# Value products of the sample tokens: one wide matmul per token row in place of three 32-column tiles

## The reference, cut to what matters

```python
s = jnp.einsum('btgrd,bgtnjd->btgrnj', q, kvg[..., 0, :]) * scale
p = _masked_softmax(s.reshape(B, G, T, R, k_top * SEL_BLOCK), smask)...
o_s = jnp.einsum('bgtrnj,bgtnjd->btgrd', p.astype(q.dtype), kvg[..., 1, :])
...
o_w = jnp.einsum('btgrl,blgd->btgrd', p.astype(q.dtype), kvw[:, :, 1])
o = g[..., 0:1] * o_c + g[..., 1:2] * o_s + g[..., 2:3] * o_w
```

## Time and profile before

| | before |
|---|---|
| median of 3 runs | 933.69 us |
| the profiled execution | 941.16 us, its span 939.4 us |
| TensorE busy (matmul records) | 833.3 us, 89% |
| VectorE, ScalarE, POOL busy | 341.7, 269.6, 108.9 us |
| TensorE's share of the chain that ended last | 83% |
| mean granted TensorE clock | 0.915 |

### The profile page before, as it was taken

How to read it: one execution, slowest core, us unless ns; L and a number is a source line. 1 busy time by engine, 2 the same in 40 slices (tenths; PEclk the granted TensorE clock), 3 DMA queues, 4 the chain that set the end, 5 groups by cost and what they waited for, 6 DMA issues and landing times.

```text
span 939.4 us, 16800 instructions
## 1 busy us (share of the span) xinstructions
PE 833.3 (89%) x7021; PEld 550.3 (59%) x7021; DVE 341.7 (36%) x774; ACT 269.6 (29%) x713; POOL 108.9 (12%) x178
## 2 busy tenths in 40 slices
PE   0899999999997999989999787898968779887996
PEld 0455666666664655778784454565646667654441
DVE  0133133333333111432030364666646346433433
ACT  0135323332333000011120354565713323333211
POOL 1200600000000000000000383111131112000000
PEclk9999799999998999968999988999975876877998
DMA  9949703333000222320451016000062656520121
GB/s 229 374 195 334 287 1 135 134 134 134 0 0 1 73 71 89 93 89 2 143 220 67 7 55 284 2 2 1 1 236 76 248 192 221 208 78 31 45 79 33
DMA packets 34407, 108.09 MB, mean 115 GB/s; under 512 B 5667, under 2 KB 14930, under 8 KB 33187
## 3 DMA queue, kind: packets, MB, share of 16 engines
q1 hardware_dynamic: 28579, 56.77, 17.9%
q0 software_dynamic: 5760, 50.33, 14.2%
HBM read 101.80 MB, written 11.55 MB: 121 GB/s over the span
## 4 chain that ended last, share of the span: by engine, by line
PE 83%; DVE 6%; ACT 4%; issue 3%; SPq 2%; another core or an unknown queue 1%; DMA 0%; POOL 0%; ACTq 0%; DVEq 0%; POOLq 0%
PE ps L862 18%; PE ps L1007 13%; PE ps L1275 7%; PE ps L1005 7%; PE ps L1161 5%; PE ps L848 4%; PE ps L1061 3%; PE ps L1110 3%; PE ps L1185 3%; PE ps L1201 2%; PE ps L1085 2%; PE ps L1012 2%; PE ps L973 1%; SPq L651 1%; PE ps L808 1%
## 5 line engine op out<-in xcount | busy, mean ns | idle before, releaser
L862 PE MATMUL ps<-xt,w 128*128 128x381 f32 x512 | 175.1, 488 | 0.7 <-DVE xt L1286 0.7
L1007 PE MATMUL ps<-wcols,hT 128*128 128x384 f32 (+3 forms) x384 | 123.8, 483 | 2.1 <-DVE hT L1642 2.1
L862 PEld LDWEIGHTS ps<-xt,w 128*128 128x128 f32 x512 | 93.7, 192 | 53.6 <-issue 1.4
L1007 PEld LDWEIGHTS ps<-wcols,hT 128*128 128x128 f32 x384 | 74.0, 194 | 48.7 <-issue 30.1
L1285 DVE COPY xt<-ps 64x384 f32<-64x384 f32 x64 | 35.3, 551 | 154.9 <-PE ps L848 154.8
L1275 PE MATMUL ps<-w_o,mixT 128*128 128x512 f32 (+1 forms) x160 | 70.6, 600 | 0.0
L1161 PE MATMUL ps<-kt,qs 32*32 32x128 f32 x1920 | 51.4, 354 | 18.8 <-issue 14.2
L1285 ACT COPY xt<-ps 64x384 f32<-64x384 f32 x64 | 30.2, 472 | 124.3 <-PE ps L848 121.9
L1005 PE MATMUL ps<-hT,wcols 128*128 128x288 f32 x256 | 64.5, 413 | 0.7 <-ACT z_gate L1334 0.7
L848 PEld LDWEIGHTS ps<-ident,cache 128*128 128x128 f32 x384 | 46.2, 144 | 22.9 <-issue 13.9
L1161 PEld LDWEIGHTS ps<-kt,qs 32*32 32x32 f32 x1920 | 43.2, 129 | 27.9 <-issue 20.1
(11 more groups left out here) (290 smaller groups left out, 1004.8 us busy)
## 6 DMA issues: line engine op xcount, KB each, us to landing
wcols<-in_w_ada SPq DMA_DIRECT2D x6, 2048.0 KB, 10.7
wcols<-in_w_in SPq DMA_DIRECT2D x4, 2048.0 KB, 8.5
win_rows<-in_state_win_kv SPq DMA_DIRECT2D x8, 768.0 KB
out<-in_state_win_kv SPq DMA_DIRECT2D x1, 6048.0 KB
wcols<-in_w_in SPq DMA_DIRECT2D x2, 1536.0 KB, 12.0
w_o<-in_w_out SPq DMA_DIRECT2D x1, 3072.0 KB, 11.5
w<-in_phi_w SPq DMA_DIRECT2D x4, 512.0 KB, 9.7
x_rows<-in_x_prompt SPq DMA_DIRECT2D x1, 2048.0 KB, 8.8
```

The costliest lines, as they stand in the source:

```text
L862: last = pe.matmul(ps[:, 4 + k, 0:G * NC].rearrange("p (g n) -> p g n", g=G), w1[:, m * JP + s - 1, k, :], xt[(s - 1) % NXT][:, k * G:(k + ...
L1007: last = pe.matmul(ps[:, job_bank[j], 0:width], hT[:, c, t * P:(t + 1) * P], w[:, c, col:col + width], **flags)
```

## The change

`sample_values` makes one matmul for each token row j: all 96 columns of `pt` are the weights, and the 192 value columns of the three groups are streamed at once. The result in PSUM is 96 x 192 for each branch: the rows of group g against the values of all three groups, of which only the block of group g is wanted. The selected branch stands in columns 0:192 of bank 7, the window branch in 192:384. The new tokens take one matmul with 384 columns, and `new_v` is laid out to fit, so that each of its DMAs writes rows of 192 values in place of three pieces of 64. `finish_sample` reads the diagonal blocks, each of 32 rows by 64, with three instructions in place of L1812 and three in place of L1814.

```diff
-                    sp.dma_start(new_v[u][n * TS:(n + 1) * TS, :, n * d:(n + 1) * d], rows[b, :, 1]).then_inc(win_in[u], 16)
+                    sp.dma_start(new_v[u][n * TS:(n + 1) * TS, n, :], rows[b, :, 1].rearrange("t g d -> t (g d)")).then_inc(win_in[u], 16)
...
-                values, at0 = (win_rows[b % NBUF], d) if late else (kv_rows[(b * (NCH - 1) + c) % NROW], 0)
+                values, at0 = (win_rows[b % NBUF], G * d) if late else (kv_rows[(b * (NCH - 1) + c) % NROW], 0)
                 for j in range(4):
-                    for g in range(G):
-                        v0 = KV // 2 + g * d
-                        last = pe.matmul(ps[g * SQ:(g + 1) * SQ, 7, at0:at0 + d], pt[n % NPT][:, j, g * SQ:(g + 1) * SQ],
-                                         values[:, j, v0:v0 + d], start=(c == 0 and j == 0), stop=False, skip_group_check=True)
+                    last = pe.matmul(ps[0:GR, 7, at0:at0 + G * d], pt[n % NPT][:, j, :], values[:, j, KV // 2:],
+                                     start=(c == 0 and j == 0), stop=False, skip_group_check=True)
                 if late:
-                    for g in range(G):
-                        last = pe.matmul(ps[g * SQ:(g + 1) * SQ, 7, 0:2 * d], pt[n % NPT][0:2 * TS, 4, g * SQ:(g + 1) * SQ],
-                                         new_v[b % NBUF][:, g, :], start=False, stop=True, skip_group_check=True)
+                    last = pe.matmul(ps[0:GR, 7, 0:2 * G * d], pt[n % NPT][0:2 * TS, 4, :],
+                                     new_v[b % NBUF][:].rearrange("p n c -> p (n c)"), start=False, stop=True, skip_group_check=True)
                 last.then_inc(pt_used, 1)
...
-                own_step.done(dve.scalar_tensor_tensor(out=out_rows[u][:], in0=ps[0:GR, 7, 0:d], scalar=coef[:, 2:3],
-                                                       in1=cmp_out[:, b, :], op0=ALU.mult, op1=ALU.add))
-                dve.scalar_tensor_tensor(out=out_rows[u][:], in0=ps[0:GR, 7, d:2 * d], scalar=coef[:, 3:4],
-                                         in1=out_rows[u][:], op0=ALU.mult, op1=ALU.add).then_inc(out_made, 1)
+                for g in range(G):
+                    of = slice(g * SQ, (g + 1) * SQ)
+                    last = dve.scalar_tensor_tensor(out=out_rows[u][of], in0=ps[of, 7, g * d:(g + 1) * d], scalar=coef[of, 2:3],
+                                                    in1=cmp_out[of, b, :], op0=ALU.mult, op1=ALU.add)
+                own_step.done(last)
+                for g in range(G):
+                    of = slice(g * SQ, (g + 1) * SQ)
+                    last = dve.scalar_tensor_tensor(out=out_rows[u][of], in0=ps[of, 7, (G + g) * d:(G + g + 1) * d],
+                                                    scalar=coef[of, 3:4], in1=out_rows[u][of], op0=ALU.mult, op1=ALU.add)
+                last.then_inc(out_made, 1)
```

More of the change, by code:

```diff
@@ L321, in program @@
         win_rows = [at(f"win_rows{u}", [P, WJ, KV], win_at[u]) for u in range(NBUF)]
-        new_v = [at(f"new_v{u}", [2 * TS, G, 2 * d], win_at[u] + WJ * KV * 4) for u in range(NBUF)]
+        new_v = [at(f"new_v{u}", [2 * TS, 2, G * d], win_at[u] + WJ * KV * 4) for u in range(NBUF)]
         gate_dram = nc.dram_tensor("gate_dram", [NS, 3 * H], F32).ap()
```

## The result

The changed kernel takes 946.5 us (four runs, 945.85 to 949.22), the kernel before 932.54 us by its four runs. The ratio is 1.0155, with a 95% interval of 1.0119 to 1.019. It is slower, as forecast, by 14 us and not by 6.

What follows compares the result with a forecast made beforehand. TensorE was taken as the bound: 21 us of work added, 9.3 back from pauses and 6 from the clock, total +5.7, giving 939.4 us on the median (ratio 1.0061). Own range 933 to 946, with rivals 927 to 960.

Steps and rivals of the forecast that it cites:

- The bound: Whole stage: TensorE bounds it, so what the change does to TensorE goes to the end unless something covers it.
- Price of a value chunk: Values on TensorE: a chunk takes 1.30 us in place of 0.58 at full clock, 2.56 in place of 1.00 at half.
- Work added: Each round on TensorE: 3.9 us more per sequence, part of it filling waits, +2.8 net a round.
- The pattern round: Round from 792.01, with one clock fall: 14.21, less 0.4, plus 2.8, gives 16.6 us; six of them 99.6.
- The pauses: In the scores, TensorE out of instructions behind DMA bursts: three of four go, one of 2.5 us stays; 9.3 come back.
- The clock: Rounds of the stage: dense value streams raise the granted clock, one fall a round; 6 us come back.
- DVE and DMAs: Four more DVE instructions a sequence, 1.1 us at most, covered by waits for scores; new_v's DMAs and SP's, POOL's waits cost nothing.
- The last stretch: From 822.80 to 838.00: seventh round's 9.9 us become 10.4, the last sequence's 5.2 become 8.8; +4.1.
- Rival 3: Scores: the pauses stay, with half of the clock's return lost; +18, or 951.5 us; chance 0.11.
- Rivals 1 and 4: Stage: clock stays 1.00 and all four pauses go, 930.9 us, chance 0.22; values beside something misread, nothing moves, 934, chance 0.05.
- rival 2: Rounds: the clock falls as often as now and the values meet it; +25, or 958.5 us; chance 0.17.

Runs made afterwards that it cites:

- e3: Changed kernel with matmuls put back to three 32-column tiles, keeping the new PSUM and new_v layout and six DVE instructions: 930.78 us.
- e1: Changed kernel with a quarter of the bytes in each gather from the 15th on: 934.86 us, 1.0021 of the kernel before.
- e2: Kernel before with a quarter of the bytes in each gather from the 15th on: 918.93 us, 0.9857 of the kernel before.
- e7: Kernel before with the 4 MB of output weights issued behind sequence 6's second value chunk, not ahead of the scores of 7: 926.67 us, 0.9943.
- e9: Kernel before with the output weights issued behind sequence 6's second value chunk, measured once more with five rounds: 928.4 us, 0.9951.
- e10: Changed kernel with the output weights issued behind sequence 6's second value chunk: 944.52 us, 1.0129 of the kernel before.
- e4: Changed kernel with values 0 and 1 and turns 2 and 3 of the last sequence issued inside the scores: 942.93 us, 1.0128.
- e5: Changed kernel with values 0, 1 and turns 2, 3 inside the scores, and DVE joining a sequence straight behind the key transposes: 939.22 us, 1.0078.
- e11: Changed kernel with the wide matmul in chunks 0 and 1 alone, the rest in three narrow tiles: 945.75 us, 1.0137 of the kernel before.
- e12: Changed kernel with chunks 0 and 1 in three narrow tiles, chunks 2 to 4 and new tokens wide: 943.09 us, 1.0116 of the kernel before.
- e6: Kernel before with values 0, 1 and turns 2, 3 moved inside the scores and DVE's joining moved earlier: 949.28 us, 1.0169.
- e8: Repeat, in one look, of the changed kernel with values inside the scores and DVE joining earlier: 936.06 us.

## Why the prediction was right and wrong

**The bound, right.** The chain stayed TensorE's, and everything that the change did to it in this stage arrived at the end.

**Price of a value chunk, right.** 1.30 us at full clock, as worked out from the dense stream of rows 6. New tokens take 0.81 in place of the 0.65 expected, and the transposes behind a wide chunk 0.33 in place of 0.48, so that chunk and turn are 1.63 and not 1.78. The section is 8.65 us for the 8.8 predicted. The Trainium skill (TensorEngine Tiling (Array Packing), Key Properties) says that changing the tiling mode drains TensorE. The 0.15 us by which the pair is cheaper than the sum said is in the direction of that rule; no run here separates it from other causes.

**Work added, right.** From values 0 to the start of the next scores a round needs 10.45 us at nearly full clock (805.12 to 815.57) and 7.58 in e3 (779.30 to 786.88): +2.9 for the 2.8 predicted. What the stage grew by, with pauses and clock in it, is 19.8 us against e3 (119.1 to 138.9), for the 5.7 predicted; the span grew by 20.3 (927.2 to 947.5), the time by 15.7 (930.78 to 946.5).

**The pattern round, right in its total, by luck.** 16.6 us predicted, 16.36 measured, in the one round without a pause. The values' section was taken at 8.8 and took 10.13 (788.76 to 798.89), for its first chunk was at half clock; the rest was taken at 7.8 and took 6.23, for its scores were not. The two errors cancel. The forecast took six such rounds and got one.

**The pauses, wrong.** This is the step that failed: three of four pauses should go, because 168 instructions fewer and a later start of the scores would let the blocks in. "9.3 come back from pauses" was its term. None came back: 16.0 us in five pauses after, against 14.6 in e3 and 11.8 in the execution of rows 7. Against e3 that is 10.7 of the 14.1 us by which the stage's growth was forecast too low. The mechanism was right in part: light gathers took most of each pause away (e1, e2), the moved load of the weights took 1.6 us or more of the last (e7, e9, e10), and spreading the same instructions took most of them away (e4, e5).

Two things were wrong. The first is shown: the burst was not "nearly over by then". Over the 6 us ahead of each of the four pauses behind gathers the DMA engines of the changed kernel are 92 to 98% busy. The gathers, released later by the longer values, were still running under the scores. The second is an argument from counts: the saved instructions lie in the wrong stretch. A block is 16 KiB: 0.77 MB in 47 packets. The Trainium skill (Runtime: NRT & Kernel Launch, Instruction fetch mechanics) gives 256 instructions for it, and that agrees with the packets falling from 52 to 47 for 1,344 instructions fewer. In the changed kernel one instruction packet moves between 735.0 and 742.5 us; TensorE gets through 461 matmuls and weight loads from 735.0 on and stops at 743.01. The scores alone are 480, so that with no more than that in hand a block has to come while they run, however slowly the values in front of them use theirs. The change thinned out the stretch that had no pause and left the one that had. That section of the Trainium skill calls crossing a block mostly hidden. From 0 to 690 us TensorE's matmuls wait 2.9 us for "issue", which agrees; the 16.0 us in the scores don't.

**The clock, right in size as far as an estimate tells.** It did come back: 0.89 over the stage against 0.80 in e3 and 0.77 in the execution of rows 2. Six rounds grew by 13.0 us against e3. The added work is 6 x 2.9 = 17.4 and the pauses are 1.4 longer, so 5.8 came back by something else, and "6 from the clock" was the forecast. It came in other places than expected: the scores gained, and behind each remaining pause stands a wide chunk at half clock that takes 2.8 us, where a narrow one takes 1.00. This is an estimate from comparing rounds; no run held the clock fixed.

**DVE and DMAs, right.** Six joining instructions of 0.28 us each, as the bound from above had it:

```profile
L1811 DVE SCALAR_TENSOR_TENSOR out_rows<-ps,coef,cmp_out 32x64 f32<-32x64 f32 x24 | 6.6, 277 | 23.5 <-PE ps L1202 23.3
```

They cost nothing that can be measured (e3), and TensorE waited for them 0.3 us once. The cover was real: in e4, where the joining comes too late for values 0, TensorE waited 5.8 us for it.

**The last stretch, too small.** +4.1 predicted to the end of the values, +6.8 against e3 (14.8 to 21.5 us). The last sequence's part is 3.4 for the 3.6 worked out. The seventh round's was taken at 0.5 and is 3.4 as well (9.5 to 12.9 us): its first two chunks meet the half clock behind the pause that stays, 2.80 and 2.02 us in place of 1.30.

**The base.** The rounds were read from an execution whose part ahead of the stage was late by 6 to 12 us. That changed no term of the sum, which goes by differences, and its stage is as long as e3's.

**The rivals.** Rival 3 (the pauses stay) is the nearest to what happened, put at +18 in spans and 951.5 us with a chance of 0.11; the measured span difference is 20.3 (to e3) and the time 946.5. Its other half, pauses that have nothing to do with DMA or with instructions, doesn't fit e1, where fewer bytes, and e5, where another order took most of them away. Rivals 1 and 4 are ruled out by the time, rival 2 by the clock of 0.89.

The timed medians put the price at 14 to 16 us and the profiled spans at 20.3. Most of that gap is in the choice of executions: the changed kernel's profiled one is 2.7 us above its median, e3's 1.75 below. What stays open is why two wide chunks cost what five do. e11 and e12 bound it (9 us of added work cost 15, 12 us cost 12, with intervals that overlap) but don't say how the clock's fall is decided. How many instructions are held ahead was not tested by a run of its own.

## What to carry to other kernels

Narrow tiles side by side in the array are worth what their overlap says (here 24 ns a record against 56): a wide matmul that computes three times what is wanted saves instructions and costs the array's time, and where TensorE is the bound that is the bill. Before counting fewer instructions as a gain, look at which stretch runs out of them; taking them from another stretch returned nothing here. And look for large loads that fall on the stretch which is densest in instructions: moving one by some 9 us gave 0.5% here, at no cost.

## What the runs showed of the hardware that was not expected

- The pauses in the scores behind gathers are 2.6 to 3.4 us in the changed kernel, with DMA engines 92 to 98% busy over the 6 us ahead of each. In the scores of sequence 7 of e7, e9 and e10, with DMA engines 3% busy over the same 6 us, there is none over 0.9 us.
- TensorE, busy without a gap for 41 us with value tiles of 32 columns, was granted 0.50 throughout (e6), and 1.00 over 32 us when the value tiles were 96 columns wide in the same order (e5): being busy was not what brought the clock back.
- Two executions of one kernel had the same seven rounds to within 0.25 us, pauses and half clock included (e5, e8); two of another differed by up to 1.7 us in a round (e7, e9).
